# The first head of an attention stage: its query quads in ascending order, and a score lead that grows from 32 to 72 tile columns

## The chip, the cores and the metric

One kernel runs on one core of a Trainium2 chip. The metric is the device time of one execution in microseconds; each kernel is run several times and the median counts. The core has five engines that run their own instruction streams and meet at semaphores: TensorE (PE, with its weight loads shown apart as PEld), VectorE (DVE), ScalarE (ACT), GpSimd (POOL) and SyncE (SP), which here only issues transfers.

## What is computed

A decoder layer on 2048 tokens of width 1024: RMS norm, differential attention with 8 heads, a residual, a mixture of experts, a last RMS norm. The change touches the attention alone:

```python
rel = qpos[:, None] - kpos[None, :]
bias = rel_table[t5_bucket(rel)].transpose(2, 0, 1)
s = einsum('ibhqd,ibhkd->ibhqk', q, k) * scale + bias      # i = 0, 1: two score maps
s = where(rel >= 0, s, -inf)
p = softmax(s, axis=-1)
a = p[0] - lam * p[1]
o = einsum('bhqk,bhkd->bhqd', a, v)
```

Everything before it (the projection, which writes q, k and v to memory) and after it (output projection, routing, experts) is the same in both kernels.

## The kernel before, in words

`attend` treats 8 heads one after the other. A head has 2048 queries in 16 **rows** of 128 queries; row i sees (i+1)·128 keys (causal), so rows are 128 to 2048 columns wide. Four rows make a **quad** j = 0 to 3. A quad of index j has 4j+4 **units**: unit k is the column of 128 keys number k. Line 324, `QUADS = (2, 0, 3, 1)`, sets the order of the quads in every head. In that order the rows are numbered r = 0, 1, 2 and so on over all heads, and in the changed kernel the same numbers mean other rows: before, r = 0 to 3 of the first head are 1152 to 1536 wide, r = 4 to 7 are 128 to 512, r = 8 to 11 are 1664 to 2048, r = 12 to 15 are 640 to 1024.

A row is scored in pieces (lines 331 to 336), for each of its two maps one piece up to 1024 columns, or two: a rest of 128 to 1024 columns and one of 1024. What a piece goes through:

- PE scores it (`score`, L652): two matmuls for each 512 columns, in float32r, into one of two buffers of `ps_s`, in turn. Piece c waits until DVE has taken piece c-2.
- DVE takes it (`take`, L581 for far keys, L584 for the last 256 with their bias) from `ps_s` into a ring in SBUF (`p0_ring` for the first map, `p1_ring` for the second) with the running maximum. The first piece of a row waits until the ring has room (L573, L576: `turned` of an older quad, `mixed` of an older row).
- ACT raises each map of the row (L546, exponential and sum), 0.4 to 2.0 us each.
- DVE writes the row's weight (`weigh`: L605, L610, the tile `coef`), which has to wait for both exponentials.
- POOL multiplies the second map by it (L516) and adds it to the first (L518, `mixed`).
- When all four rows of a quad are mixed, PE turns its units one by one: `turn` (L672) transposes up to four 128x128 tiles into `ps_t` (only four minus the tiles above the diagonal: the last units of a quad have 3, 2, 1), ACT copies them out (L535), and two slots later `add_v` (L687) multiplies with v. After a quad its output is turned back (L695) and stored.

**The plan.** All engines follow one list of slots n, made at build time (lines 348 to 397). Slot n holds unit n, and the score pieces that keep the scored columns ahead of the turned ones by LEAD tile columns (units of 256 score columns in the plan's count; one tile of a unit counts one). With LEAD = 72 the plan begins at slot -18: 18 slots with scores only, then unit 0. Within a slot PE's order is scores, turn, add_v of unit n-2, turn back; DVE's is takes, output, weights; ACT's is the copy of the unit, then exponentials. Each engine works strictly in this order, so a wait holds all that stands behind it. `exps` (377 to 386) puts the exponentials of a row from the slot after its last piece on, and no further map once 640 has been spent in a slot (a map costs half its width plus 128); `coefs` puts the weight one slot after the second map.

SP's list: q of a quad is loaded (L463) into one of two buffers once the quad two before it has been scored; k and bias of a head two heads later, v likewise.

Of the kernel before, what the change touches and what calls it, by code (L numbers as in the profile page):

```python
# [18 lines left out]
HEADS = 8  # L19
# [299 lines left out]
def attend(nc, io, keep, scratch, sem):  # L319
# [1 line left out]
    SCALE = HALF ** -0.5  # L321
    NEAR = 2 * P
    WIDE = 1024
    QUADS = (2, 0, 3, 1)
    LEAD = 72
    P0, P1 = 70 * 256, 24 * 256
    A_RING, V_LAG = 4, 2

    quads = [(h, j) for h in range(HEADS) for j in QUADS]
    rows = [(g, 4 * j + a) for g, (h, j) in enumerate(quads) for a in range(4)]  # L330
    pieces = []
    for r, (g, i) in enumerate(rows):
# [5 lines left out]
    NG, NR, NC, NU = len(quads), len(rows), len(pieces), len(units)  # L338
# [5 lines left out]
    def tiles(u):  # L344
        g, k = units[u]
        return 4 - max(0, k - 4 * quads[g][1])

    BEGIN, END = -LEAD // 4, NU + 8
    slots, c, scored_cost, turned_cost = {}, 0, 0.0, 4 * BEGIN
    for n in range(BEGIN, END):  # L350
        start = c
        while c < NC and scored_cost < turned_cost + LEAD:
            scored_cost += pieces[c][3] / (2 * P)
            c += 1
        slots[n] = range(start, c)
        turned_cost += tiles(n) if 0 <= n < NU else 4
# [20 lines left out]
    exps, soon, e_slot = {}, [], {}  # L377
    for n in range(BEGIN, END):
        soon += [(r, m) for r in range(NR) if slot_of[last_piece[r]] == n - 1 for m in range(2)]
        spent = 0  # L380
        exps[n] = []
        while soon and (spent < 640 or n >= NU):
            r, m = soon.pop(0)
            exps[n].append((r, m))
            spent += (rows[r][1] + 1) * P // 2 + 128
            e_slot[r] = n
# [1153 lines left out]
def build(nc, io, out):  # L1540
    with ExitStack() as ctx:
# [31 lines left out]
        project(nc, io, keep, scratch, sem)  # L1573
        keep["wo_raw"] = keep["p1_ring"][:, 0:KC // 2 * D].rearrange("p (c n) -> p c n", c=KC // 2)
        attend(nc, io, keep, scratch, sem)
        k0.close()
        with nc.sbuf_tensor("gu_raw", [P, 2, GS, GC, 2, FF], F32) as gu_raw:
# [43 lines left out]
```

## Time and profile before

| | us |
|---|---|
| median of 3 runs | 2635.84 (2632.71 to 2638.82) |
| the profiled execution, its own time | 2649.18 |
| its span, first to last instruction | 2647.6 |
| projection, until the attention's first load | 603 |
| attention: first score at 624.57, head 2's first unit at 759.35 | 134.8 |
| each later head, for example 759.35 to 846.18 | 86.8 |
| attention ends, later stages follow | about 1345 |

Over the whole span PE is busy 89%, DVE 52%, ACT 46%, POOL 27%. In a timeline a row is: start in us, duration, engine, line, operation, output<-input, shapes, count, and in brackets the time that the engine sat idle before it and who ended that. PE's busy share counts matmuls that wait in its pipeline too, so distances between starts say more than busy time. PEclk is the clock that TensorE was granted, as a share of 2.4 GHz: 0.50 is the level of 1.2 GHz.

### The profile page before, as it was taken

The numbers are of one execution on the slowest core, as the hardware profiler recorded it, in microseconds if no ns is written. First come the engines' busy times: TensorE is split into PE (matmuls) and PEld (weight loads), VectorE is DVE, ScalarE is ACT, GpSimd is POOL, SyncE is SP. The second block draws the span as 40 slices with busy tenths as digits, with TensorE's granted clock in tenths as the row PEclk, the third lists the DMA queues.
The fourth block names the chain that finished last, engine by engine and source line by source line (L and its number), as shares of the span: only waits on it lengthen the run. The fifth ranks groups of instructions, "written<-read, shape, count | busy, mean of one in ns | idle before, by whom it ended". The sixth has DMA issues, their size and how long they took to land. (4 is left out here: it accounts for less than half of the span.)

```text
span 2647.6 us, 36772 instructions
## 1 busy us (share of the span) xinstructions
PE 2348.6 (89%) x11480; PEld 1879.0 (71%) x11480; DVE 1380.5 (52%) x2803; ACT 1218.1 (46%) x1642; POOL 725.7 (27%) x558
## 2 busy tenths in 40 slices
PE   4999999995999999999958999479999999999981
PEld 3888889993666666666637777356788888788760
DVE  6212121003667666666633666557665555666663
ACT  5011111112666666666642444246554555556553
POOL 0000000002776666675620011122222222222220
PEclk7999999995899999999978899689999999999995
DMA  5333334215334433442143423279889788888867
GB/s 183 135 111 127 111 131 113 62 46 143 78 83 110 106 95 80 110 102 69 40 138 121 163 106 111 79 251 356 313 277 302 225 285 270 274 291 311 304 187 269
DMA packets 207628, 441.45 MB, mean 167 GB/s; under 512 B 19081, under 2 KB 56113, under 8 KB 205490
## 3 DMA queue, kind: packets, MB, share of 16 engines
q1 hardware_dynamic: 187186, 375.27, 42.3%
q0 software_dynamic: 19008, 60.91, 9.2%
q10 hardware_dynamic: 1344, 4.19, 0.7%
q8 instruction: 42, 0.69, 0.1%
q14 instruction: 48, 0.39, 0.0%
HBM read 338.55 MB, written 101.76 MB: 166 GB/s over the span
## 5 line engine op out<-in xcount | busy, mean ns | idle before, releaser
L1371 DVE TENSOR_TENSOR gu_lo<-gu_raw,gu_hi 128x2048 fp32r<-128x2048 f32 x128 | 293.3, 2291 | 131.8 <-issue 79.1
L581 DVE TENSOR_SCALAR_CACHE_REDUCE p_ring<-ps_s 128x256 f32<-128x256 f32 (+7 forms) x352 | 277.8, 793 | 158.8 <-PE ps_s L652 153.8
L518 POOL TENSOR_TENSOR p_ring<-p_ring 128x1152 f32<-128x1152 f32 (+15 forms) x128 | 321.9, 2515 | 10.7
L546 ACT ACTIVATE p_ring<-p_ring,shift 128x1152 f32<-128x1152 f32 (+15 forms) x256 | 306.0, 1197 | 29.2 <-DVE shift L597 29.2
L687 PE MATMUL ps_o<-aT,v_st 128*128 128x512 f32 (+3 forms) x640 | 291.9, 540 | 0.0
L535 ACT ACTIVATE aT<-ps_t 128x512 f32<-128x512 f32 (+1 forms) x320 | 168.1, 531 | 227.7 <-PE ps_t L672 227.7
L652 PE MATMUL ps_s<-k,q_st 128*128 128x512 f32 (+3 forms) x640 | 214.5, 464 | 44.2 <-DMA near<-near_rows 24.6
L1312 ACT ACTIVATE gu_hi<-gu_raw 128x2048 fp32r (+1 forms) x128 | 237.9, 1915 | 30.6 <-DMA block_table<-tab 18.0
L1444 PE MATMUL ps_g<-gu_hi,xT_lo 128*128 128x512 f32 x720 | 235.3, 408 | 7.5 <-DVE xT_lo L1386 7.5
L1444 PE MATMUL ps_g<-gu_lo,xT_hi 128*128 128x512 f32 x720 | 227.1, 397 | 0.0
L1444 PE MATMUL ps_g<-gu_hi,xT_hi 128*128 128x512 f32 x720 | 226.8, 396 | 0.0
L516 POOL TENSOR_SCALAR p_ring<-p_ring,coef 128x1152 f32<-128x1152 f32 (+15 forms) x128 | 150.5, 1176 | 258.9 <-DVE coef L610 256.1
L652 PE MATMUL ps_s<-k_st,q_st 128*128 128x512 f32 (+3 forms) x640 | 200.7, 436 | 12.5 <-DVE top L584 12.0
L652 PEld LDWEIGHTS ps_s<-k,q_st 128*128 128x128 f32 x640 | 126.7, 212 | 113.3 <-issue 38.4
L672 PE MATMUL ps_t<-ident,p_ring 128*128 128x128 f32 x1088 | 178.5, 281 | 26.0 <-POOL p_ring L518 26.0
L1379 DVE TENSOR_TENSOR d_lo<-d_raw,d_hi 128x2048 fp32r<-128x2048 f32 x64 | 146.7, 2293 | 84.0 <-ACT d_hi L1319 68.4
L672 PEld LDWEIGHTS ps_t<-ident,p_ring 128*128 128x128 f32 x1088 | 138.2, 144 | 69.8 <-POOL p_ring L518 27.9
L238 DVE TENSOR_TENSOR stage<-ps,stage 128x512 fp32r<-128x512 f32 x64 | 44.3, 692 | 274.6 <-ACT stage L185 274.6
L185 ACT ACTIVATE stage<-ps 128x512 fp32r<-128x512 f32 x64 | 38.2, 597 | 313.6 <-PE ps L301 313.6
L1279 POOL DMA_INDIRECT x_rows<-y_sb,lists x45 | 98.4, 2187 | 284.6 <-ACT y_sb L1330 270.6
L652 PEld LDWEIGHTS ps_s<-k_st,q_st 128*128 128x128 f32 x640 | 115.2, 191 | 78.5 <-issue 43.9
L1340 ACT ACTIVATE act_g<-ps_g 128x512 f32<-128x512 f32 x45 | 27.0, 600 | 291.2 <-PE ps_g L1444 291.2
(215 smaller groups left out, 4311.3 us busy)
## 6 DMA issues: line engine op xcount, KB each, us to landing
gu_raw<-in_moe_w_gate SPq DMA_DIRECT2D x128, 512.0 KB, 9.1
gu_raw<-in_moe_w_up SPq DMA_DIRECT2D x128, 512.0 KB, 10.8
d_raw<-in_moe_w_down SPq DMA_DIRECT2D x64, 1024.0 KB, 7.9
qk<-stage SPq DMA_DIRECT2D x64, 512.0 KB, 2.8
q_st<-qk SPq DMA_DIRECT2D x128, 256.0 KB, 5.1
w_raw<-in_diff_w_in POOLq DMA_DIRECT2D x12, 1024.0 KB, 6.8
k<-qk SPq DMA_DIRECT2D x8, 1024.0 KB, 12.3
v<-stage SPq DMA_DIRECT2D x64, 128.0 KB, 1.8
```

Source lines behind the costliest of these rows:

```text
L516: pool.tensor_scalar(p1(r, 0, w), p1(r, 0, w), coef[:, r % 8, :], 0.0, ALU.mult, ALU.add).then_inc(scaled, 1)
L518: pool.tensor_tensor(p0(r, 0, w), p0(r, 0, w), p1(r, 0, w), ALU.add).then_inc(mixed, 1)
L535: nc.scalar.activation(aT[:, n % A_RING, a0 * P:], ps_t[:, turn_of["T", n] % 2, a0 * P:], ACT.Copy).then_inc(t_out, 1)
L546: nc.scalar.activation(p, p, ACT.Exp, bias=shift[:, r % 8, m:m + 1], accum_out=sums[:, r % 8, m:m + 1]).then_inc(raised, 1)
L581: ins = nc.vector.tensor_scalar(p(r, k0, k0 + far), ps_s[:, c % 2, 0:far], SCALE, None, ALU.mult, ALU.max, accum_out=top[:, r % 4, m, col: ...
L652: mm = pe.matmul(ps_s[:, c % 2, j:j + e], q_st[:, g % 2, hl, m, a * P:(a + 1) * P], k_st[h % 2][:, m, k0 + j:k0 + j + e], start=hl == 1, s ...
L672: mm = pe.transpose(ps_t[:, t % 2, a * P:(a + 1) * P], p0(4 * g + a, k * P, (k + 1) * P), ident[:, :])
L687: pe.matmul(ps_o[:, g % 2, a0 * P:], v_st[:, h % 2, k, :], aT[:, u % A_RING, a0 * P:], start=k == 0, stop=last).then_inc(summed, 1)
L1312: nc.scalar.activation(gu_hi[:, j * GC:(j + 1) * GC], raw(half, j), ACT.Copy).then_inc(gu_hi_set, 1)
L1371: nc.vector.tensor_tensor(gu_lo[:, j * GC:(j + 1) * GC], raw(half, j), gu_hi[:, j * GC:(j + 1) * GC].bitcast(F32), ALU.subtract).then_inc( ...
L1379: nc.vector.tensor_tensor(d_lo[:, j * DC:(j + 1) * DC, :], d_raw[:, j], d_hi[:, j * DC:(j + 1) * DC, :].bitcast(F32), ALU.subtract).then_i ...
L1444: mm = pe.matmul(ps_g[:, half, :], x[:, cs], w[:, c, half, :], start=c == 0 and k == 0, stop=c == KC - 1 and k == 2)
```

## The change

The first head takes its quads in the order 0, 1, 2, 3 and all others in the order (2, 0, 3, 1) as before. The lead is 32 tile columns until slot 0 and grows by 4 a slot to 72 at slot 10; the plan begins at slot -8. Up to slot 18 the limit on exponentials in a slot is 1400 in place of 640.

```diff
-    QUADS = (2, 0, 3, 1)
-    LEAD = 72
+    QUADS = ((0, 1, 2, 3),) + ((2, 0, 3, 1),) * (HEADS - 1)
+    LEAD0, LEAD = 32, 72
...
-    quads = [(h, j) for h in range(HEADS) for j in QUADS]
+    quads = [(h, j) for h in range(HEADS) for j in QUADS[h]]
...
-    BEGIN, END = -LEAD // 4, NU + 8
+    BEGIN, END = -LEAD0 // 4, NU + 8
...
-        while c < NC and scored_cost < turned_cost + LEAD:
+        while c < NC and scored_cost < turned_cost + min(LEAD, LEAD0 + 4 * max(0, n)):
...
-        while soon and (spent < 640 or n >= NU):
+        while soon and (spent < (640 if n > LEAD // 4 else 1400) or n >= NU):
```

Worked through, the plan's lists differ until slot 38 and are the same from slot 39 on: at that point both have scored the same pieces and turned the first head. In the changed plan the scores of slots -7 to 0 are the rows of 128 to 1024 columns (r = 0 to 7); slots 1 to 10 hold the rows r = 8 to 13 in pairs of a small and a 1024 piece, two such pieces of 1024 in slots 1, 2 and 7. The quads start at slots 0, 4, 12 and 24 (before: 0, 12, 16 and 32). The weights are in these slots: r = 3 in -3, r = 7 in 3, r = 11 in 9, r = 12 in 10, r = 13 in 12, r = 15 in 22.

## Rows read from the trace of the kernel before

**Rows 1.** Windows: stretch, its length, busy of PE, PEld, DVE, ACT, POOL, PEclk, DMA.
```profile
624.57:669.76 45.19, 34.85 (x88) 23.72 (x89) 29.85 (x116) 17.93 (x35) 21.79 (x15) 0.58 0.47 118
669.76:703.76 34.00, 30.75 (x145) 21.99 (x143) 23.10 (x72) 24.39 (x41) 25.49 (x11) 0.95 0.16 37
703.76:759.35 55.59, 52.45 (x241) 37.39 (x241) 37.86 (x135) 35.53 (x68) 35.04 (x24) 0.95 0.47 108
759.35:846.18 86.83, 80.49 (x394) 57.00 (x392) 60.03 (x204) 59.46 (x109) 59.02 (x32) 1.00 0.41 99
```

**Rows 2.** Timeline of PE, the scores ahead of unit 0.
```profile
624.57 3.03 PE L652 MATMUL ps_s<-k,q_st 128*128 128x128 f32 x8 [24.55 <-DMA near<-near_rows]
628.47 2.50 PE L652 MATMUL ps_s<-k,q_st 128*128 128x512 f32 x6 [0.88 <-DVE top L584]
...
652.83 5.85 PE L652 MATMUL ps_s<-k,q_st 128*128 128x128 f32 x14 [1.08 <-DVE top L584]
659.01 2.84 PE L652 MATMUL ps_s<-k,q_st 128*128 128x512 f32 x12 [0.33 <-DMA q_st<-qk]
...
666.01 1.65 PE L652 MATMUL ps_s<-k,q_st 128*128 128x512 f32 x4 [2.51 <-DVE p_ring L581]
...
669.76 1.05 PE L672 MATMUL ps_t<-ident,p_ring 128*128 128x128 f32 x4
```

**Rows 3.** Timeline of PE, a slot with a 256 and a 1024 piece.
```profile
718.65 1.86 PE L652 MATMUL ps_s<-k_st,q_st 128*128 128x256 f32 x6
720.35 0.60 PE L672 MATMUL ps_t<-ident,p_ring 128*128 128x128 f32 x4
720.78 1.02 PE L687 MATMUL ps_o<-aT,v_st 128*128 128x512 f32 x2
721.24 1.86 PE L652 MATMUL ps_s<-k_st,q_st 128*128 128x256 f32 x6
```

**Rows 4.** Timeline of PE, waits inside the head and what follows them.
```profile
703.76 1.11 PE L672 MATMUL ps_t<-ident,p_ring 128*128 128x128 f32 x4 [3.25 <-POOL p_ring L518]
...
710.33 1.02 PE L687 MATMUL ps_o<-aT,v_st 128*128 128x512 f32 x2
...
745.20 0.87 PE L652 MATMUL ps_s<-k_st,q_st 128*128 128x512 f32 x4 [0.76 <-DVE top L584]
...
749.02 1.19 PE L652 MATMUL ps_s<-k_st,q_st 128*128 128x512 f32 x4 [1.64 <-DVE top L584]
...
793.27 0.66 PE L672 MATMUL ps_t<-ident,p_ring 128*128 128x128 f32 x4 [3.24 <-POOL p_ring L518]
```

**Rows 5.** Windows of PE alone: length, busy, PEclk, DMA share, GB/s.
```profile
650.00:658.00 8.00, 6.68 (x19) 0.50 0.58 133
...
666.00:672.00 6.00, 5.76 (x17) 0.50 0.00 0
...
704.00:709.00 5.00, 5.00 (x18) 0.50 0.01 3
```

**Rows 6.** Timeline of POOL and DVE: a weight written while L518 runs, a take.
```profile
744.82 3.44 POOL L518 TENSOR_TENSOR p_ring<-p_ring 128x1536 f32<-128x1536 f32 x1
745.23 3.05 DVE L610 SCALAR_TENSOR_TENSOR coef<-sums,neg_lam,inv 128x1 f32<-128x1 f32 x1
...
750.38 0.95 DVE L581 TENSOR_SCALAR_CACHE_REDUCE p_ring<-ps_s 128x768 f32<-128x768 f32 x1
...
751.25 0.42 DVE L584 CUSTOM_DVE_ANT_0 p_ring<-ps_s,near 128x256 f32<-128x256 f32 x1
```

**Rows 7.** Groups by shape, POOL: busy us, mean ns of one | idle before.
```profile
L518 POOL TENSOR_TENSOR p_ring<-p_ring 128x2048 f32<-128x2048 f32 x8 | 36.2, 4522 | 0.7
...
L518 POOL TENSOR_TENSOR p_ring<-p_ring 128x1024 f32<-128x1024 f32 x8 | 19.0, 2375 | 0.7
...
L516 POOL TENSOR_SCALAR p_ring<-p_ring,coef 128x2048 f32<-128x2048 f32 x8 | 15.9, 1982 | 11.5 <-DVE coef L610 11.5
...
L516 POOL TENSOR_SCALAR p_ring<-p_ring,coef 128x1024 f32<-128x1024 f32 x8 | 9.0, 1122 | 27.5 <-DVE coef L610 27.4
```

## The prediction, made before the changed kernel ran

> **What bounds the kernel now.** I read the windows by stage first. The attention begins at 624.57 us with PE's first score, and from 759.35 on (the plan's slot 40) both kernels follow the same lists. So only these 134.8 us can change, and everything later is moved as a whole; the attention's end is on the path of the whole kernel, since the stages after it need all heads. The stretch ahead of unit 0 takes 45.19 us at a granted clock of 0.58, and there PE is busy 34.85 us, DVE 29.85 and POOL 21.79; the later head of 86.83 us has PE busy 80.49 us at 1.00 [rows 1]. PE sets the pace in the head; ahead of unit 0 it is a loop: PE scores a 1024 piece, DVE takes it, and as small and 1024 pieces alternate over two buffers, all the big ones share one buffer and wait for each other. The timeline shows a period of 3.48 us for a pair there (a run of 6 matmuls, 2.50 us, behind a wait of 0.88 us for DVE) [rows 2], against 1.70 us from the first score to the transpose for a pair at full clock [rows 3].
>
> **Method.** Both plans give PE the same matmuls up to slot 40. I price this work at full clock and without waits, and then compare only what is lost on top. A head is 86.83 us less its waits, 3.24 us for POOL and some 3.3 us around the burst of small pieces (0.59, 0.76 and 1.64 us of waits, the last two in the rows, and slower starts) [rows 1, 4]: 80.3 us. The scores ahead of unit 0 are 8 pairs at 1.70, 8 small pieces at about 0.55, two pieces of 640 and 1024 at 2.37 together and one at 1.1 (distances of the kind in [rows 3]): 23.8 us. Work: 104.1 us.
>
> **Lost before.** Ahead of unit 0: 45.2 - 23.8 = 21.4. Units 0 to 2 at the low clock: 1.5. The wait for POOL at 703.76: 3.25 [rows 4]. The low clock behind it: from that transpose to the third unit's add_v are 6.57 us [rows 4], three transposes at 0.43, two scores of 1024 at 1.33, and add_v's of 2 and 1 tiles at 0.12 a tile are 4.3: 2.2. The burst: 3.3. Sum 31.7, and 134.8 - 31.7 = 103.1, within 1 us of the work above.
>
> **Lost after, part by part.**
>
> The lead to unit 0. Rows r = 0 to 3 are now 128 to 512 wide. The same eight pieces took 6.2 us before (652.83 to 659.01) [rows 2]. DVE starts at 626.5 at the earliest, as before, so PE is through them at 632.7. Then six pieces of 640 to 896, where DVE paces: takes of 0.95 to 1.2 us by the rows of a take [rows 6], and one weight in nearly each slot, 0.4 us plus what it waits for POOL (next part), 0.3 to 0.9 us. That makes about 8 us to the point where r = 7's first piece can be scored, 1.4 us, and unit 0 is turned at 642.5 in place of 669.76. Rows 0 to 3 are mixed at about 641 (weight of r = 3 at 639, POOL 2.0 us), so POOL is not the last. 17.9 us for 12.4 us of work: lost **5.5**.
>
> Slots 0 to 3. Five 1024 pieces in one buffer. The loop of PE 1.33 and DVE 1.24 us [rows 3, 6] needs 2.7 us for each, and PE has only 1.8 to 2.5 us of other work with it: lost **4.5**, slot 3 ends at 657.0.
>
> Slot 4 waits for r = 7. Its weight stands in slot 3 behind r = 9's takes, and comes 1.9 us after PE's last score there; then POOL needs 1.12 + 2.38 us [rows 7], to 662.0. PE has r = 10's pair to score and then stands: **3.3** with what the slot loses.
>
> The weights and POOL. In the trace a weight that comes while POOL is in L518 ends when L518 ends: issued at 745.23, it lasts 3.05 us, L518 ran from 744.82 to 748.26 [rows 6]. DVE stands for that time, and so do the takes and, a piece later, PE. The Trainium skill, page "SBUF — State Buffer", section "Who interferes with whom", states that a VectorE instruction with two SBUF inputs and a GpSimd one that reads SBUF exclude each other for the whole instruction; by that rule the trace's wait is a lock, and faster weights can't pass it. The changed plan packs the rows r = 7 to 13 into 10 slots while POOL needs 3.5 to 5.8 us a row, so the lock bites in slots 4, 5 and 10. I walked slots 5 to 12 with PE 2.6 us for a pair slot [rows 3]: 2.6 us are lost by takes that wait for `mixed` of r = 10 (its weight is late, behind slot 7's two 1024 pieces), and slot 12 waits **2.1** for r = 11 (weight at 681.5, POOL 5.05 us, 686.6): together **4.7**.
>
> Slot 24, the start of the widest quad. Before, units of another quad lay between its last row and its first unit, and the wait was still 3.25 and 3.24 us [rows 4]. Now r = 15's second exponential is in slot 21, its weight in slot 22 behind a pair's takes, and slots 22 and 23 hold 3 tiles. From the end of slot 22's scores: takes and weight 1.7, POOL 1.98 + 4.52 [rows 7] and gaps, 8.3 us; PE has 1.2 us to do. Lost **7.1**, the largest new wait, and **2.2** of low clock behind it, as at 703.76 [rows 4, 5].
>
> The burst of small pieces, slots 32 to 36: the same weights meet the same L518, in slots of 4 tiles: **2.2** (before 3.3).
>
> Clock. The stall at slot 4 is 2.8 us of idle PE. A wait of 2.51 us before was followed by 6 us at 0.50 [rows 2, 5], one of 3.24 us at 793 by none [rows 4]. I take the low clock for slots 5 to 7, at the 2.2 us of rows 4 and a little: **2.5** (bounds 0 and 3). For slots 0 to 3 the bounds are 0 and 3.8 (five pieces at 2.1 us in place of 1.33, the difference of the 3.48 us loop to 2.7). I take 0, because the dense run of the eight small pieces is what lifted the clock in the trace: 0.50 until 658 and a faster run from 659.01 [rows 2, 5]. Taking the middle would add 1.9.
>
> The limit of 1400 costs nothing: ACT is at most 3.8 us a slot pair against 4.4 us of PE, and its copies are needed two slots later. q loads: quad 2's is issued some 10 us ahead of its first score, the wait of 0.33 us at 659.01 [rows 2] goes. SP's other loads keep their distance of 20 slots and more.
>
> **Sum.** 5.5 + 4.5 + 3.3 + 4.7 + 7.1 + 2.2 + 2.2 + 2.5 = 32.0 us lost after, 31.7 before: +0.3 us. The 27 us that unit 0 gains are given back in slots 0 to 24. The profiled execution of 2649.18 us would become 2649.5; on the median of the runs, 13.3 us lower, 2635.84 + 0.3, rounded to **2636**.
>
> **Rivals.**
>
> Forecast: no difference, 2630.6 to 2641.1 (a measurement of this kernel can tell about 0.2%, 5.3 us, from no change; this bound holds for all three chances). Chance 0.42.
>
> Faster: DVE isn't the pace of the early stretch. If takes and weights run beside PE as well as in the later heads, the loop's 4.5 shrinks to 1, the 4.7 of slots 5 to 12 to 1, and without the clock's 2.5 the sum is 22.3: -9.4 us, 2626. For it: DVE is busy only 60 of 87 us in a head [rows 1]. Against: the loop is plain in rows 2. Chance 0.33.
>
> Slower: the lock. If the weights of r = 12 and r = 13 both meet L518 of the row before (3.8 us at widths of 1664 to 1792), slots 12 to 15 lose two waits of 3.05 us [rows 6], +6.1 and +0.3: 2642. In my walk r = 13's weight comes 0.3 to 0.5 us before that L518 starts; it decides from there. Against: PE waits for POOL at slot 12 anyway, which hides one of them. With the low clock in slots 0 to 3 as well it is +10, 2646. Chance 0.25. The Trainium skill, same page and section, makes no exception for GpSimd's one-input operation; by that rule L516 would hold a weight too, up to 1.98 us more at a row [rows 7], and this rival would be likelier.
>
> That the change does not start unit 0 earlier at all I leave out: its transposes need only k, q and the ident, which the first scores had [rows 2], and their own four rows; v is needed two slots later.
>
> **Range.** 2623 to 2647: the faster case with 3 us more, the slower one with both parts. Faster 0.33, same 0.42, slower 0.25.
>
> **What would show it.** Right: unit 0's transpose near 642; waits of PE for POOL's L518 at slots 4, 12 and 24, the last near 7 us; L610 of 1 to 3 us between 640 and 690; slot 40 near 759. [...] Wrong: unit 0 later than 650 (then the lead isn't paced by DVE as I have it), slot 24's wait below 4 us, or a time of the attention that differs while slot 40 doesn't.

## The result

| | before | changed |
|---|---|---|
| median of 8 runs, us | 2637.62 (2632.37 to 2646.44) | 2648.18 (2639.48 to 2653.83) |
| ratio | | 1.0031, 95% interval 1.0016 to 1.0046 |
| profiled execution, its time | 2649.18 | 2647.54 |
| its span | 2647.6 | 2646.0 |
| first score to slot 40 | 134.78 | 139.07 |
| first score to the last transpose of the attention | 737.0 | 744.0 |

The changed kernel is slower by 0.31%, some 8 us. The forecast was worked out from a median before of 2635.84; with the ratio that makes 2644.0, inside the stated range of 2623 to 2647. The median of the eight runs, 2648.18, lies 1.2 us above it. Either way it isn't the likeliest case (no difference) but the one with a chance of 0.25. The two profiled executions don't show the difference in their spans, since that of before lies 11.6 us above its own median (2649.18 against 2637.62), and its stages behind the attention took 8 us longer (1288.3 us from the last unit turned to the end, against 1280.3); so I compare the attention, and above all the stretch up to slot 40. The page of the changed kernel begins:

```profile
span 2646.0 us, 36770 instructions
## 1 busy us (share of the span) xinstructions
PE 2341.2 (88%) x11480; PEld 1872.7 (71%) x11480; DVE 1383.5 (52%) x2803; ACT 1219.1 (46%) x1642; POOL 706.4 (27%) x558
```

The windows of the changed kernel, cut where its quads start (slots 0, 4, 12, 24) and at slot 40, answer to [rows 1]; columns as there:

```profile
623.98:642.94 18.96, 14.50 (x45) 10.18 (x45) 12.92 (x66) 8.69 (x25) 5.63 (x8) 0.64 0.87 227
642.94:663.48 20.54, 12.76 (x49) 8.58 (x48) 15.78 (x54) 8.52 (x16) 11.67 (x8) 0.92 0.20 51
663.48:690.57 27.09, 24.68 (x100) 17.28 (x100) 18.56 (x56) 16.92 (x26) 17.82 (x8) 0.87 0.21 49
690.57:724.24 33.67, 25.24 (x117) 17.03 (x117) 19.18 (x54) 19.55 (x29) 23.89 (x9) 0.98 0.46 101
724.24:763.05 38.81, 36.66 (x165) 26.27 (x166) 24.90 (x88) 24.45 (x47) 21.24 (x14) 0.93 0.27 66
```

The lead to unit 0 fell from 45.19 to 18.96 us, and PE lost the 26 us again: it is busy only 12.76 of 20.54 us in slots 0 to 3, and 25.24 of 33.67 in slots 12 to 23. The timeline of PE in the changed kernel names the waits (answers to [rows 2, 4]):

```profile
633.29 6.45 PE L652 MATMUL ps_s<-k,q_st 128*128 128x512 f32 x20 [1.88 <-DMA q_st<-qk]
...
642.94 0.66 PE L672 MATMUL ps_t<-ident,p_ring 128*128 128x128 f32 x4
...
646.83 0.41 PE L652 MATMUL ps_s<-k,q_st 128*128 128x128 f32 x2 [1.60 <-DVE top L584]
...
663.48 0.66 PE L672 MATMUL ps_t<-ident,p_ring 128*128 128x128 f32 x4 [3.04 <-POOL p_ring L518]
...
683.77 0.96 PE L652 MATMUL ps_s<-k,q_st 128*128 128x512 f32 x4 [1.29 <-DVE p_ring L581]
...
697.40 1.20 PE L652 MATMUL ps_s<-k,q_st 128*128 128x512 f32 x4 [1.67 <-DVE top L584]
...
724.24 1.12 PE L672 MATMUL ps_t<-ident,p_ring 128*128 128x128 f32 x4 [6.62 <-POOL p_ring L518]
...
763.05 0.60 PE L672 MATMUL ps_t<-ident,p_ring 128*128 128x128 f32 x4
```

The 6.62 us before slot 24 come about as a chain over three engines. The timelines of ACT, DVE and POOL of the changed kernel show r = 15, 2048 columns wide: its second exponential, its weight, and the sum over the whole row, behind which PE starts at 724.24:

```profile
713.92 2.00 ACT L546 ACTIVATE p_ring<-p_ring,shift 128x2048 f32<-128x2048 f32 x1
...
717.31 0.22 DVE L610 SCALAR_TENSOR_TENSOR coef<-sums,neg_lam,inv 128x1 f32<-128x1 f32 x1
...
717.63 1.98 POOL L516 TENSOR_SCALAR p_ring<-p_ring,coef 128x2048 f32<-128x2048 f32 x1 [4.65 <-DVE coef L610]
719.69 4.49 POOL L518 TENSOR_TENSOR p_ring<-p_ring 128x2048 f32<-128x2048 f32 x1
```

And two weights of the changed kernel met L518 of the row before, as in [rows 6] (POOL's rows, then DVE's):

```profile
687.07 3.45 POOL L518 TENSOR_TENSOR p_ring<-p_ring 128x1536 f32<-128x1536 f32 x1
...
692.37 3.74 POOL L518 TENSOR_TENSOR p_ring<-p_ring 128x1664 f32<-128x1664 f32 x1
...
688.53 2.00 DVE L610 SCALAR_TENSOR_TENSOR coef<-sums,neg_lam,inv 128x1 f32<-128x1 f32 x1
...
693.98 2.15 DVE L610 SCALAR_TENSOR_TENSOR coef<-sums,neg_lam,inv 128x1 f32<-128x1 f32 x1
```

688.53 + 2.00 is 690.53, and 687.07 + 3.45 is 690.52; 693.98 + 2.15 is 696.13, and 692.37 + 3.74 is 696.11.

L516, POOL's other instruction, holds a weight too. Here the first pair is of the changed kernel, the second of the run `order_alone` below; 760.30 + 0.41 and 760.23 + 0.49 meet within 0.01 us, and so do 644.73 + 0.75 and 644.68 + 0.80:

```profile
760.23 0.49 POOL L516 TENSOR_SCALAR p_ring<-p_ring,coef 128x256 f32<-128x256 f32 x1 [1.71 <-DVE coef L610]
...
760.30 0.41 DVE L610 SCALAR_TENSOR_TENSOR coef<-sums,neg_lam,inv 128x1 f32<-128x1 f32 x1
...
644.68 0.80 POOL L516 TENSOR_SCALAR p_ring<-p_ring,coef 128x640 f32<-128x640 f32 x1
...
644.73 0.75 DVE L610 SCALAR_TENSOR_TENSOR coef<-sums,neg_lam,inv 128x1 f32<-128x1 f32 x1
```

Such holds are few. A weight that started within 0.02 us after L516's own start took its usual 0.22 us (at 636.41 in the changed kernel, L516 at 636.40).

### The profile page after: what moved, and what is told of

Read it like the earlier page. It is cut to its first block and busy times, and to the rows that moved or that the text cites. A ratio compares the mean times of both kernels' runs of the same rounds, so it can differ in the third digit from the quotient of the medians.

```text
span 2646.0 us, 36770 instructions
## 1 busy us (share of the span) xinstructions
PE 2341.2 (88%) x11480; PEld 1872.7 (71%) x11480; DVE 1383.5 (52%) x2803; ACT 1219.1 (46%) x1642; POOL 706.4 (27%) x558
## 5 line engine op out<-in xcount | busy, mean ns | idle before, releaser
L581 DVE TENSOR_SCALAR_CACHE_REDUCE p_ring<-ps_s 128x128 f32<-128x128 f32 (+7 forms) x352 | 277.7, 793 | 161.2 <-PE ps_s L652 151.6
L518 POOL TENSOR_TENSOR p_ring<-p_ring 128x896 f32<-128x896 f32 (+15 forms) x128 | 322.0, 2516 | 10.7
L546 ACT ACTIVATE p_ring<-p_ring,shift 128x128 f32<-128x128 f32 (+15 forms) x256 | 305.8, 1197 | 10.6 <-DVE shift L597 10.6
L652 PE MATMUL ps_s<-k,q_st 128*128 128x512 f32 (+3 forms) x640 | 206.2, 448 | 46.9 <-DMA near<-near_rows 24.3
L516 POOL TENSOR_SCALAR p_ring<-p_ring,coef 128x896 f32<-128x896 f32 (+15 forms) x128 | 151.0, 1179 | 265.1 <-DVE coef L610 261.9
L652 PEld LDWEIGHTS ps_s<-k,q_st 128*128 128x128 f32 x640 | 120.6, 203 | 112.9 <-issue 39.4
L1279 POOL DMA_INDIRECT x_rows<-y_sb,lists x45 | 80.1, 1781 | 315.1 <-ACT y_sb L1330 298.2
## 6 DMA issues: line engine op xcount, KB each, us to landing
gu_raw<-in_moe_w_up SPq DMA_DIRECT2D x128, 512.0 KB, 10.8
```

What stands on the lines that cost most here:

```text
L516: pool.tensor_scalar(p1(r, 0, w), p1(r, 0, w), coef[:, r % 8, :], 0.0, ALU.mult, ALU.add).then_inc(scaled, 1)
L518: pool.tensor_tensor(p0(r, 0, w), p0(r, 0, w), p1(r, 0, w), ALU.add).then_inc(mixed, 1)
L546: nc.scalar.activation(p, p, ACT.Exp, bias=shift[:, r % 8, m:m + 1], accum_out=sums[:, r % 8, m:m + 1]).then_inc(raised, 1)
L581: ins = nc.vector.tensor_scalar(p(r, k0, k0 + far), ps_s[:, c % 2, 0:far], SCALE, None, ALU.mult, ALU.max, accum_out=top[:, r % 4, m, col: ...
L652: mm = pe.matmul(ps_s[:, c % 2, j:j + e], q_st[:, g % 2, hl, m, a * P:(a + 1) * P], k_st[h % 2][:, m, k0 + j:k0 + j + e], start=hl == 1, s ...
```

## The experiments

Two theories: A, the loss sits where the last row of a wide quad meets the quad's first unit, with POOL's time on that row in the middle; B, it is the lock of weights by L518 in the dense slots. "Window" is the time from the first score to slot 40, before 134.78, changed 139.07. Ratios are to the kernel before, with their 95% interval. "Changed" as the base means the diff is on the changed kernel.

**The order alone.** `LEAD = 72` and the limit of 640 as before, `QUADS[0] = (0, 1, 2, 3)`.

> The order (0, 1, 2, 3) in the first head with the old lead of 72 and the old limit of 640. Theory A (the losses lie where the last row of a wide quad meets its first unit, because row, exponential, weight and the 2048 wide POOL work follow each other within two slots): unit 0 near 665 us, no wait for POOL at slots 4 and 12, but the wait at slot 24 stays at 6.6 us, because r = 15 is scored in slots 16 to 19 as in the changed kernel; slot 40 at 763 within 2 us, the ratio to before +0.1 to +0.4%. Theory B (the losses lie in the dense slots 1 to 12, where weights meet POOL's L518): with the scores spread over the lead those slots are calm, slot 40 comes at 757 or before and the kernel is at least as fast as before.

Ratio 1.0025 (1.0013 to 1.0036), window 137.62. Unit 0, slot 24 and slot 40 in its timeline of PE:

```profile
670.66 1.06 PE L672 MATMUL ps_t<-ident,p_ring 128*128 128x128 f32 x4
...
724.21 1.11 PE L672 MATMUL ps_t<-ident,p_ring 128*128 128x128 f32 x4 [6.61 <-POOL p_ring L518]
...
762.92 0.60 PE L672 MATMUL ps_t<-ident,p_ring 128*128 128x128 f32 x4
```

As A has it: no wait for POOL at slots 4 and 12, the same 6.6 us at slot 24, and slot 40 as late as in the changed kernel. B had said 757. The window is 2.8 us longer than before, and its one wait for POOL 3.4 us longer (6.61 against 3.25 us). Unit 0 came 5.6 us later than I expected. In absolute time slot 40 comes within 0.2 us of the changed kernel's, whether unit 0 comes at 643 or at 671; counted from the first score, which came at 625.30 here, it comes 1.4 us sooner.

**The lead alone.** The old order can't start at 32, as its first quad would need a weight of slot 3 at slot 0; 56 is possible.

```diff
-    QUADS = ((0, 1, 2, 3),) + ((2, 0, 3, 1),) * (HEADS - 1)
-    LEAD0, LEAD = 32, 72
+    QUADS = ((2, 0, 3, 1),) * HEADS
+    LEAD0, LEAD = 56, 72
...
-        while soon and (spent < (640 if n > LEAD // 4 else 1400) or n >= NU):
+        while soon and (spent < 640 or n >= NU):
```

> The old order (2, 0, 3, 1) with the lead starting at 56 and growing by 4 a slot to 72, limit 640 (with the old order a start at 32 can't work: the weight of r = 3 would stand in slot 3, behind unit 0). Theory A: the first quad (r = 0 to 3, 1152 to 1536 wide) is mixed near 665.2 us as before, so unit 0 comes at most 4.5 us earlier, near 665, and 1 to 4 us are left at slot 40 (756 to 758); no wait at POOL over 4 us. Theory B: the denser slots 0 to 4 cost what the start gains, slot 40 at 759 to 761.

Ratio 1.0020 (1.0007 to 1.0033), window 135.87. Its PE:

```profile
663.51 1.12 PE L672 MATMUL ps_t<-ident,p_ring 128*128 128x128 f32 x4 [2.48 <-POOL p_ring L518]
...
706.26 0.66 PE L672 MATMUL ps_t<-ident,p_ring 128*128 128x128 f32 x4 [3.35 <-POOL p_ring L518]
...
760.73 0.60 PE L672 MATMUL ps_t<-ident,p_ring 128*128 128x128 f32 x4
```

Unit 0 is 6 us earlier than before, and slot 16 is 2.5 us later. An earlier start is given back with the old order as well. For slot 40 A had said 756 to 758, which 760.73 misses by 2.7 us; B's 759 to 761 holds, and one weight (at 689.70) is held for 3.44 us. A's other sign, no wait for POOL over 4 us, holds. Of the 6.3 us at unit 0, 0.8 are left at slot 4 (677.79 against 678.57), by when the scores moved behind unit 0 are done; slot 40 is 1.4 us late. The run sides with B on slot 40 and doesn't separate what cost the rest.

**The limit of 1400 up to slot 24,** `(640 if n > 24 else 1400)` on the changed kernel.

> The changed kernel with the limit of 1400 kept up to slot 24, so that both exponentials of r = 15 stand in slot 20 and its weight in slot 21. Theory A: the weight comes 2.1 us earlier, the wait of PE for POOL before slot 24 goes from 6.6 to about 4.5 us and slot 40 comes 2 us earlier than in the changed kernel, at 761. Theory B: the wait at slot 24 shrinks, but the weight of r = 16 then meets L518 of r = 15 and slot 40 does not move.

Ratio 1.0033 (1.0021 to 1.0046), window 141.93. The wait is shorter, slot 40 isn't earlier:

```profile
667.00 0.66 PE L672 MATMUL ps_t<-ident,p_ring 128*128 128x128 f32 x4 [3.03 <-POOL p_ring L518]
...
728.47 1.11 PE L672 MATMUL ps_t<-ident,p_ring 128*128 128x128 f32 x4 [5.25 <-POOL p_ring L518]
...
767.23 0.60 PE L672 MATMUL ps_t<-ident,p_ring 128*128 128x128 f32 x4
```

1.4 of the expected 2.1 us went from the wait. B's event came as well: the weight of r = 16, issued at 724.80 while L518 of r = 15 ran, lasted 3.63 us; but slots 24 to 40 took no longer for it (38.76 us against 38.81). 2.2 us were lost before slot 4, in slots whose plan is the same. There the granted clock was lower than in the changed kernel's profile (0.92), and it was so in two more of the runs below with the same plan up to slot 18. The windows of PE and the others for slots 0 to 3, columns as in [rows 1], of this run, of the one with less POOL time on r = 15 and of the one with halves:

```profile
644.26:667.00 22.74, 15.03 (x50) 10.09 (x49) 15.78 (x54) 8.62 (x16) 11.65 (x8) 0.77 0.19 46
...
645.25:667.88 22.63, 15.13 (x50) 10.16 (x49) 15.78 (x54) 8.62 (x16) 11.63 (x8) 0.77 0.19 46
...
642.45:664.87 22.42, 16.38 (x50) 11.10 (x49) 14.36 (x54) 8.62 (x16) 10.24 (x9) 0.70 0.20 47
```

So the changed kernel's profile, with 20.54 us there, is a favourable one by some 2 us. The run decides neither for A nor for B, and the total shows no gain.

**POOL's time on r = 15.** `w = P if r == 15 else (i + 1) * P` in POOL's loop of the changed kernel: for one row POOL mixes 128 columns and leaves out the other 1920, so the output of that row isn't the layer's.

> The changed kernel, in which POOL mixes only the first 128 columns of r = 15 (2048 wide) of the first head; the other columns of that row keep the first map alone, so this part of the computation is left out, and 5.7 us of POOL's 6.6 us at that row go. Theory A (the wait before slot 24 is POOL's time on the widest row behind a weight that comes two slots before): the wait goes from 6.6 to under 1 us, the low clock behind it too, and slot 40 comes 6 to 8 us earlier than in the changed kernel, 131 to 133 us after the first score in place of 139.1; the total is then no slower than before. Rival (other waits take its place, the burst of small pieces for one): slot 40 gains under 3 us.

Ratio 0.9992 (0.9980 to 1.0004), 0.39% less than the changed kernel has; window 134.53:

```profile
723.65 0.66 PE L672 MATMUL ps_t<-ident,p_ring 128*128 128x128 f32 x4 [0.98 <-POOL p_ring L518]
...
760.50 0.60 PE L672 MATMUL ps_t<-ident,p_ring 128*128 128x128 f32 x4
```

The wait went from 6.62 to 0.98 us, and the total is that of the kernel before. In the window it is 4.5 us, less than the 6 to 8 expected. From slot 12 on it is 7.6 us (64.85 us against 72.48); the slots before it, where the edit changes nothing, took 3.1 us more, 2.1 of them in slots 0 to 3 as above. So A has the place right: POOL's time on this row, with the low clock behind it, is worth the whole difference. The same edit on the kernel before, where PE waits 3.25 us for r = 11, was not run; so this run alone doesn't show what separates the two orders. Together with the order alone it makes this row the likeliest price of the ascending order.

**The weight without the second tensor input.** On the changed kernel, and on the kernel before:

```diff
-                nc.vector.scalar_tensor_tensor(out=coef[:, r % 8, :], in0=sums[:, r % 8, 0:1], scalar=neg_lam[:, 0:1],
-                                               in1=inv[:, r % 16, 1:2], op0=ALU.mult, op1=ALU.mult).then_inc(coefed, 1)
+                nc.vector.tensor_scalar(coef[:, r % 8, :], sums[:, r % 8, 0:1], neg_lam[:, 0:1], inv[:, r % 16, 1:2],
+                                        ALU.mult, ALU.mult).then_inc(coefed, 1)
```

> The changed kernel with the weight computed by a tensor_scalar: the sum is the one tensor input, the negative lambda and the inverse are its two per-partition scalars, the same product. Theory B (a DVE operation with two tensor inputs in SBUF is held while L518 runs): no L610 is longer than 0.3 us (0.22 is the usual length; the changed kernel has 0.54 to 2.15 us in the first head), the waits of PE for DVE in the burst of small pieces of each head shrink by 1 to 2 us, slot 40 comes 3 us earlier, near 760, and the whole kernel is 0.5 to 0.7% faster than the changed one. Theory A alone: the weight is late for another reason (its exponential, the slot it stands in), lengths stay, no difference beyond 0.1%.

> The kernel before with the weight by tensor_scalar. If the lock costs each head alike, it gains as the changed kernel did from it (0.86% between the two medians): 0.5 to 0.8% faster than before. If the lock costs mainly the dense first slots of the changed order (the slower rival of the prediction), this kernel gains less than the changed one did, and the distance between the two orders without the lock shrinks below 0.1%. First head: first score to slot 40 some 131 to 133 us (before 134.8; the changed kernel with this weight had 133.9).

On the changed kernel: ratio 0.9946 (0.9926 to 0.9967), window 133.85. On the kernel before: 0.9917 (0.9899 to 0.9935), window 128.61. Both gains are above what I expected (0.85% for 0.5 to 0.7, 0.83% for 0.5 to 0.8), and the second window is shorter than its 131 to 133. The line's summary in the changed kernel with it (minimum, median, maximum in ns), and one weight inside an L518 that ran from 641.74 to 643.03:

```profile
L610 DVE TENSOR_SCALAR coef<-sums,neg_lam,inv x128: 271/273/278, 636.2 to 1319.9; 128x1 f32<-128x1 f32 x128
...
641.93 0.27 DVE L610 TENSOR_SCALAR coef<-sums,neg_lam,inv 128x1 f32<-128x1 f32 x1
...
641.74 1.29 POOL L518 TENSOR_TENSOR p_ring<-p_ring 128x512 f32<-128x512 f32 x1
```

No weight is held any more (the longest was 3.43 us). So the lock is real and costs 0.8% of the whole kernel. But it costs both orders about the same: 0.9946/1.0031 is 0.9915 for the changed one, 0.9917 for the old one, and the distance between the orders stays 0.29%, where B needed it under 0.1%. By my estimate from the two intervals it lies between 0.0 and 0.6%, so the times alone don't rule B out; but the windows are 5.2 us apart without the lock and 4.3 with it. B is not borne out as the reason for the difference.

**The loads of k and v behind q and bias.** Changed kernel, and both edits on the kernel before:

```diff
             load_q(sp, 1)
+            load_v(sp, 0)
+            load_k(sp, 1)
             load_near(sp, 1)
+            load_v(sp, 1)
...
-            load_k(act, 1)
-            load_v(act, 0)
-            load_v(act, 1)
```

> The changed kernel with the loads of k of the second head and of v moved from ACT's queue behind the q and bias loads on SP's. The first score waited 24.3 us for the bias (near) and the fifth piece 1.9 us for q of the second quad. If these waits are the 3 MB of k and v that were issued first, the first score comes at 611 to 615 in place of 624.0, the wait for q goes, and the kernel is 8 to 13 us (0.3 to 0.5%) faster than the changed one; if they are the latency of the loads themselves, nothing moves. Unit 0 to slot 40 as in the changed kernel.

> The kernel before with both: the weight by tensor_scalar and the loads of k and v behind q and bias. If the two are independent, the gains add: 0.9 to 1.2% faster than before, 2606 to 2614 us.

On the changed kernel: ratio 0.9998 (0.9984 to 1.0013), 0.33% under the changed kernel, at the lower end of what I expected. The first score comes at 610.00, and then a new wait takes most of it:

```profile
610.00 6.27 PE L652 MATMUL ps_s<-k,q_st 128*128 128x128 f32 x16 [10.80 <-DMA near<-near_rows]
...
641.35 2.50 PE L652 MATMUL ps_s<-k,q_st 128*128 128x128 f32 x6 [13.60 <-DMA q_st<-qk]
```

q of the third quad is issued only at 630.83, behind k, v and the two transfers of zeros in SP's queue, which the short lead now needs at once. The old order reaches that q later: there both edits together give 0.9863 (0.9844 to 0.9883), 2605.9 us, window 127.69; more than the 0.9 to 1.2% expected.

**The last row of a quad in two halves.** POOL works on r with r % 4 = 3 and over 512 columns in two halves and signals after the first (`early`); PE waits for the three other rows and that signal, and for the whole row at the middle unit.

```diff
+                if half:
+                    pool.tensor_scalar(p1(r, 0, half), p1(r, 0, half), coef[:, r % 8, :], 0.0, ALU.mult, ALU.add).then_inc(halved, 1)
+                    pool.wait_ge(halved, sum(1 for x in range(r + 1) if split_at(x)))
+                    pool.tensor_tensor(p0(r, 0, half), p0(r, 0, half), p1(r, 0, half), ALU.add).then_inc(early, 1)
...
+                elif half and k == half // P:
+                    pe.wait_ge(mixed, 4 * g + 4)
```

> The changed kernel in which POOL mixes the last row of each quad with j = 1 to 3 in two halves of columns, with a signal after the first; PE starts the quad's units behind the first half and waits for the whole row at the unit in the middle. The full computation. If the waits before slots 4, 12 and 24 are POOL's time on the last row, each shrinks by about half of that time: slot 4 from 3.04 to 1.3, slot 24 from 6.62 to 3.4 us, the wait of 3.25 us in each later head to 0 to 0.3, and the low clock behind them goes in most heads: 25 to 40 us off the attention, 1.0 to 1.5% off the changed kernel. If something else (ACT's exponentials, DVE) is late there as well, the waits stay above 2 us.

> The changed order with the halves and with the weight by tensor_scalar: the two together, so 0.5 to 0.9% below the version with the halves alone. Beside th_before it shows what the ascending order is worth when both known waits are smaller. If its loss was the wait at slot 24, the remaining 3.4 us there leave it at about the same time as th_before, within 0.15%.

> The old order and lead with the halves and the weight by tensor_scalar. The waits of 3.25 us in all 8 heads go, and the low clock behind them: 1.6 to 2.2% faster than before, 2580 to 2598 us.

> th_before with the loads of k and v behind q and bias, which had brought 0.5% beside the weight alone: 2.1 to 2.8% faster than before, 2566 to 2585 us.

| halves and | base | ratio (interval) | median | window |
|---|---|---|---|---|
| nothing else | changed | 0.9859 (0.9841 to 0.9877) | 2602.49 | 135.50 |
| weight | changed | 0.9799 (0.9781 to 0.9817) | 2585.86 | 128.88 |
| weight | before | 0.9775 (0.9758 to 0.9792) | 2578.04 | 124.45 |
| weight, loads | before | 0.9747 (0.9732 to 0.9762) | 2571.00 | 123.18 |

PE at slots 4 and 24 with the halves alone (the lines of kernel.py have moved: L691 is `turn`; the profile names no releaser here but "issue", and PE waits for two semaphores at this place):

```profile
664.87 0.63 PE L691 MATMUL ps_t<-ident,p_ring 128*128 128x128 f32 x4 [1.57 <-issue]
...
723.64 0.63 PE L691 MATMUL ps_t<-ident,p_ring 128*128 128x128 f32 x4 [3.65 <-issue]
```

The same line's waits in the old order with halves and weight (in all, times, longest):

```profile
PE ps_t L691 <- issue: 2.7, 8, 0.3
```

The waits came out near what POOL's time alone gives (1.3 and 3.4 expected): 3.04 to 1.57, 6.62 to 3.65, and 26.0 us in 8 waits before to 2.7. The gain is larger than expected: 1.7% off the changed kernel for 1.0 to 1.5, and 2578.04 us on the kernel before for 2580 to 2598. The old order stays ahead by 0.25% even so (0.0 to 0.5% by my estimate from the two intervals); I had expected within 0.15%. The changed order with halves and weight still has waits of 3.71 us at slot 24, 1.63 at slot 4 and 2.00 for q; the old one has 0.34 us at most for a row of POOL and 0.32 for q. The last version beats both kernels, the one before by 2.5%.

## Why the prediction came out as it did

It was right that the early start is given back, and where: at slot 4 and above all at slot 24. It was wrong that the sum comes out even. The window is 4.3 us longer where 0.3 was forecast, which is the distance between "no difference" and "slower".

- **The sum.** 104.1 us of work and 139.07 measured leave 35.0 us lost, against 32.0 forecast: 3.0 us too low. A further 1.0 us was in the comparison itself: the parts of before add up to 31.7, while the same 104.1 of work leaves 30.7 of its 134.78. The prediction saw that gap ("within 1 us") and didn't carry it.
- **Lead.** Unit 0 at 642.94 for 642.5; as the first score came 0.6 us earlier the stretch is 1.0 us longer. A step that failed: "q loads [...] the wait of 0.33 us goes". It looked at the third quad's q, and not at the second's, which is now needed 7 us after the first score in place of 28: PE waited 1.88 us for it, and 1.84 to 2.06 us in the other profiles with the ascending order and the old place of the loads.
- **Slots 0 to 3.** 20.54 us for 19.5, with slot 4's wait at 3.04 for 2.8. The prediction took the low clock in these slots at nothing (bounds 0 and 3.8). The profile of this kernel bears that out with 0.92; the three windows above, at 0.70 to 0.77, cost about 2 us more.
- **Slots 4 to 12.** 27.09 us. The prediction has 24.6 (662.0 to 686.6), and doesn't say whether its 2.5 us of low clock are in that; with them it is 27.1. The takes waited for `mixed` as said (1.29 us at 683.77), and the clock was 0.72 in 664 to 670 and 0.65 in 686 to 690. The expected wait for POOL at slot 12 (2.1 us) isn't in this profile; in four others with the same plan up to there (`late24`, `short_r15`, `coef_ts_after`, `loads_after`) it is 1.72 to 1.79 us.
- **Slots 12 to 24.** The prediction names no time for these. Here the slower rival's event happened: the weights of r = 12 and r = 13 were both held (2.00, 2.15 us) and cost PE 1.67 us at 697.40. The prediction had it as a close call and counted nothing in its sum: the second step that failed. In `late24`, `short_r15` and `loads_after` r = 13's weight was held for 3.77 to 3.78 us and PE waited 2.02.
- **Slot 24.** 6.62 us for 7.1, then 0.50 of the clock from 724 to 729 (a transpose of four took 1.12 us, as in [rows 4]). Held. The Trainium skill's page "TensorE: Matmul & The Clock Gate" advises against long idle gaps between matmul bursts in its closing table ("Why this matters for your kernels"). Behind this gap the trace agrees; of the eight waits of 3.25 us in the kernel before, the ones that end at 793.27 and 1148.28 were followed by 1.00.
- **Slots 24 to 40.** 38.81 us, 2.15 of them waits. In `short_r15`, which has the same plan there and stood at 1.00, they took 36.85: so the low clock behind slot 24 cost about 2 us, for 2.2 forecast. Held.
- **The rivals.** The faster one failed at its premise: DVE was the pace of slots 0 to 3, with waits of PE up to 1.60 us. The slower one (0.25) had the sign right, and its price (+6.4 us) is near the measured 8; in part that is luck. Its mechanism cost 1.67 us of wait and not 6.1, and the runs with the new weight don't bear it out as what separates the two kernels.

The two failed steps, 1.88 and 1.67 us, less 0.5 for the shorter wait at slot 24, come to 3.1 us, the size of the miss in the sum; what is left of the lead and of slots 0 to 3 differs by about 1 us, one down and one up.

The Trainium skill, page "SBUF — State Buffer", section "Who interferes with whom", says that a VectorE instruction with two SBUF inputs contends with a GpSimd instruction that reads SBUF. The trace agrees, for L518 (holds up to 3.43 us) and for L516 (0.41 us at 760.30, 0.75 us in `order_alone`), as the prediction read the rule; what L516's holds cost is small. The same section says that a VectorE instruction with at most one SBUF input, outside the 2-port modes, does not contend with GpSimd. The trace agrees: all 128 weights by `tensor_scalar` took 0.27 to 0.28 us on the changed kernel, 38 of them started while L518 ran and 13 while L516 did. Whether this instruction entered such a mode, no run shows.

**Open.** The window explains 4.3 us of the 8 (0.31%, interval 0.16 to 0.46%). The favourable slots 0 to 3 of the changed kernel's profile may hide some 2 us more. Past slot 40 the changed kernel's attention is 2.6 us longer, in heads with the same plan. That is within scatter: from slot 40 to the last unit turned, the seven profiles with this plan and this weight took 597.7 to 603.0 us (before 600.0, changed 602.6). The wait of 3.25 us in each head is followed by the low clock in some heads and not in others, in both kernels. Whether the change shifts that, on average over many executions, no run here shows.

## What to carry to other kernels

Here a wait at the start was only traded for other waits, in the old order and in the new one. Each quad's last row goes through DVE, ACT, DVE and POOL one after the other, and what decided was how much other work PE had between that row and its first unit, not how early unit 0 came. So put the widest row's stage well ahead of its use, or let the consumer start on a part of it: the halves brought 1.7% (0.9859 against 1.0031), the new order cost 0.3%. And look for small instructions that last far beyond their median (0.22 us median, 3.4 us maximum): what they end together with shows what held them.

## What the runs showed that I had not expected

- A 128x1 operation on DVE with two tensor inputs in SBUF cost 0.8% of the kernel by the lock; the same product with one tensor input and two per-partition scalars is 0.05 us longer (0.273 against 0.220) and never held.
- With the loads of k and v issued on ACT's queue, ahead of a bias of 128 KB on SP's, PE waited 24.3 us for its first score; with them issued behind the bias, 10.8. On SP's queue k, v and the zeros then stood ahead of the next q, and PE waited 13.6 us for it.
- The wait of 3.25 us once in each head had a price beyond itself. From slot 40 to the last unit turned, the kernel before takes 600.0 us at a mean clock of 0.97, with the new weight 581.9 at 0.98, and with the halves as well 549.0 at 1.00. The halves thus took 32.9 us off these seven heads, whose waits for POOL went from 23.1 to 2.4 us.
